# Small tables packed into one transfer, weights stored in the order they are read, early loads released one after another, and the weight scaling split over two engines

## The chip, the cores and the metric

The kernel runs on all 8 cores of one Trainium2 chip, each with its own prompt sequence and its own 16 of the 128 sample rows; the weights and constant tables are the same for all, and every core reads its own copy. A core has five engines with a queue each: PE (TensorE, matrix products into eight PSUM banks), DVE (VectorE), ACT (ScalarE), POOL (GpSimd) and SP (SyncE, which here only issues transfers). An engine runs its queue strictly in order, so an instruction that waits on a semaphore holds up all that stands behind it. Transfers are issued from SP's queue (no change of type) and from POOL's queue (those that turn f32 in HBM into bf16 on chip), and both share the core's 16 DMA engines. The metric is the device time in microseconds of the slowest core.

## The reference, cut to what matters

For 2048 prompt tokens (16 tiles of 128) after 16 learned meta tokens, and for 16 sample rows:

```python
hn   = rms_norm(h, norm_w)
proj = hn @ w_in                          # (1024) x (1024, 6144)
u, gp, q, k, v, gr = split(proj)          # six parts of 1024 columns
pool_o = group_linear(window_means(u) - u, w_pool) * pool_scale
ret_o  = retention(rotary(q), rotary(k), v)        # chunks of 128, state S
ret_y  = rms_norm_per_head(ret_o) * ret_norm_w * silu(gr)
pool_y = pool_o * silu(gp)
y = rms_norm(h + concat(pool_y, ret_y) @ w_out, final_norm_w)
```

## The kernel before

`build_program` records every piece of work with the buffers it reads and writes; `Prog.schedule` then lists the pieces per engine by a planner (ranks by remaining work, costs from small formulas, a DMA rate in `HBM`), and `Prog.place` inserts the waits. The order on each engine is therefore the planner's, and it changes when costs or dependencies change. A DMA that names a buffer among its *reads* is held until that buffer is written; this is used to hold a transfer back. `queue=` chains transfers in a fixed order.

`w_in` is read in 12 blocks of 512 columns (`load_w`, POOL's queue, 2 MB of f32 each, 1 MB on chip), in the order of `WORD`: blocks 10, 11, 6, 7, then 8, 9, 4, 5, then 2, 3, 0, 1. Blocks 0 and 1 make u, 2 and 3 gp, 4 and 5 q, 6 and 7 k, 8 and 9 v, 10 and 11 gr. Tile 0 is the sample rows and meta tokens together (48 rows); tiles 1 to 16 are the prompt.

The program has two phases. While the weights arrive, tiles 1, 0, 2, 3 and 4 (`order0`) are projected block by block (`pj_mm`, `gp_mm`), and retention (`att`) and pooling (`pool`) of tiles 1 to 3 are done in between. In this phase `norm_w` is applied to the transposed activations (`A2`, a DVE evacuation with `normw` as the scale). From tile 5 on the activations are transposed by DMA and not scaled; instead every block of `w_in_bf` is multiplied in place by `norm_w` (`fold_w`, eight DVE instructions for a block) once tiles 0 to 4 have used it, and the lower half of `w_out_bf` by `ret_norm_w` (`fold_w_out`). A projection of tile 5 has to wait for the folded block.

`w_out_bf` is used as scratch in the first phase (tiles x 1 to 3, gates, k, v), so its four blocks (`load_w_out`) are loaded when that scratch has been read, between two phases. `w_pool` and `pool_scale` are loaded to scratch (`scr`, `yT`), and one DVE multiply makes `w_pool_bf`, which `pool` needs. `outp(t)` is the output projection of a tile. After tile 5's start, each tile runs `head`, `att`, `pool`, `proj` and `outp` with PE nearly always busy.

Of the kernel before, what the change touches and what calls it, by code (L numbers as in the profile page):

```python
# [312 lines left out]
def build_program():  # L313
# [177 lines left out]
    w_in_v = w_in.rearrange("(kc p) n -> p kc n", p=128)  # L491
    w_out_v = w_out.rearrange("(kc p) n -> p kc n", p=128)

    def load_w(blk):
        dma("pool", w_in_bf[:, :, blk * 512:(blk + 1) * 512], w_in_v[:, :, blk * 512:(blk + 1) * 512],
            [], ["win%d" % blk], 1 << 21, queue="w")

    def load_w_out(b):
        dma("pool", w_out_bf[:, b * 4:(b + 1) * 4, :], w_out_v[:, b * 4:(b + 1) * 4, :],
            [], ["wo%d%s" % (i, z) for i in range(4 * b, 4 * b + 4) for z in ("", "b")], 1 << 21, queue="w")  # L500
# [715 lines left out]
```

How the kernel before makes its waits and increments, by code:

```python
        def run(e, name):  # L261
            for item in self.streams[name]:
                if item[0] == "wait":
                    e.wait_ge(self.sems[item[1]], item[2])
                else:
                    _, fn, semkey, inc = item
                    fn(e).then_inc(self.sems[semkey], inc)
```

## Time and profile before

| | us |
|---|---|
| median of 3 runs (lowest, highest) | 618.67 (618.12, 619.84) |
| the profiled execution, its time | 618.45 |
| its span (slowest core, core 5) | 616.9 |
| spans of all cores | 605.4 to 616.9 |
| PE busy, core 5 | 570.6 (93%) |
| DVE busy | 414.6 (67%) |
| ACT busy | 266.0 (43%) |
| POOL busy | 112.5 (18%) |

All times below are of core 5, in us from the start of its span. "Idle before" an instruction is what its engine waited just ahead of it, with the work that ended the wait. A landing time counts from the issue of a transfer to its completion.

### The profile page before, as it was taken

What the parts mean: (1) busy time and instruction counts of PE and PEld (TensorE: products, weight loads), DVE (VectorE), ACT (ScalarE), POOL (GpSimd) and SP (SyncE); (2) the same over time, 40 slices, a digit from 0 to 9 for tenths busy, and PEclk for the clock granted to TensorE, in tenths of its full rate; (3) what the DMA queues carried; (4) which work ended last, traced back from release to release, by engine and by line L of the source; (5) the groups of instructions that cost most, each with busy time, mean ns of one, the idle gap of its engine ahead of it and who ended that gap; (6) DMA issues with size and microseconds to landing.
All of it is one profiled execution on the core that took longest, in us unless ns stands there. A gap on an engine that the chain in (4) does not pass through costs nothing.

```text
span 616.9 us, 13819 instructions; the slowest of 8 cores (605.4 to 616.9 us)
## 1 busy us (share of the span) xinstructions
PE 570.6 (93%) x4360; PEld 313.9 (51%) x4360; DVE 414.6 (67%) x1114; ACT 266.0 (43%) x831; POOL 112.5 (18%) x131
## 2 busy tenths in 40 slices
PE   0699995999699999999999999999999999899994
PEld 0244452588354646555565646464454655455651
DVE  3349997477888755856676785867767673866463
ACT  2345463553333443343345344353644534355331
POOL 6300001121010111110011122322413310330010
PEclk9999997999899999999999999999999999999998
DMA  8999999486723542544263355575775635454621
GB/s 139 212 168 181 168 172 165 83 112 113 129 73 108 133 126 60 117 103 108 72 114 120 49 171 131 182 159 118 209 137 177 166 102 142 101 152 88 123 69 38
DMA packets 90034, 78.52 MB, mean 127 GB/s; under 512 B 56254, under 2 KB 72814, under 8 KB 89948
## 3 DMA queue, kind: packets, MB, share of 16 engines
q1 hardware_dynamic: 74524, 60.09, 39.5%
q0 software_dynamic: 15440, 17.55, 20.3%
q8 instruction: 37, 0.61, 0.4%
q14 instruction: 33, 0.27, 0.1%
HBM read 64.57 MB, written 18.41 MB: 135 GB/s over the span
## 4 chain that ended last, share of the span: by engine, by line
PE 82%; DMA 9%; DVE 3%; POOL 2%; issue 1%; another core or an unknown queue 1%; SPq 0%; DVEq 0%; POOLq 0%; ACT 0%; ACTq 0%
PE pp L588 42%; PE pp L863 20%; PE pp L603 8%; DMA w_in_bf<-w_in 6%; PE pp L837 2%; DMA w_out_bf<-w_out 2%; PE pp L929 2%; PE pp L916 1%; PE pp L818 1%; PE pp L748 1%; PE pp L707 1%; PE pp L724 1%; PE pp L750 1%; DVE w_in_bf L507 1%
## 5 line engine op out<-in xcount | busy, mean ns | idle before, releaser
L588 PE MATMUL pp<-w_in_bf,hnTs 128*128 128x512 bf16 x1120 | 260.9, 384 | 19.7 <-DMA w_in_bf<-w_in 18.2
L588 PEld LDWEIGHTS pp<-w_in_bf,hnTs 128*128 128x128 bf16 x1120 | 105.4, 99 | 144.3 <-issue 32.5
L863 PE MATMUL pp<-w_out_bf,yT 128*128 128x512 bf16 x448 | 102.2, 383 | 0.3
L623 ACT ACTIVATE F<-pp,dec 128x128 f32<-128x128 f32 (+1 forms) x216 | 61.7, 369 | 59.2 <-PE pp L588 54.1
L863 PEld LDWEIGHTS pp<-w_out_bf,yT 128*128 128x128 bf16 x448 | 43.1, 99 | 53.2 <-issue 4.0
L526 POOL TENSOR_TENSOR rs_r<-rs_r,nh 128x4 f32<-128x4 f32 x32 | 35.5, 1111 | 169.9 <-DVE rs_r L523 169.6
L603 PE MATMUL pp<-hnTs,w_in_bf 128*128 128x128 bf16 x896 | 53.5, 219 | 0.0
L603 PEld LDWEIGHTS pp<-hnTs,w_in_bf 128*128 128x128 bf16 x896 | 51.0, 98 | 3.4 <-issue 0.9
L872 ACT ACTIVATE pp<-xr 128x512 f32<-128x512 f32 x30 | 18.0, 601 | 74.5 <-DVE xr L870 64.5
L910 POOL TENSOR_TENSOR scr<-vM,ident 16x512 bf16<-16x512 bf16 x32 | 35.3, 1102 | 79.4 <-PE pp L916 76.0
L786 DVE SCALAR_TENSOR_TENSOR ry<-pp,rs_r,G 128x128 bf16<-128x128 f32 x104 | 29.2, 343 | 19.6 <-POOL rs_r L526 19.3
L870 DVE TENSOR_TENSOR xr<-xr,pp 128x512 f32<-128x512 f32 x30 | 20.6, 687 | 29.6 <-PE pp L863 29.4
L640 DVE TENSOR_TENSOR F<-F,cs 128x512 f32<-128x512 f32 x53 | 36.6, 691 | 4.7
L588 PE MATMUL pp<-w_in_bf,xr 128*128 128x512 bf16 (+1 forms) x160 | 37.7, 380 | 1.0 <-DVE xr L575 1.0
L776 ACT ACTIVATE ry<-pp 128x128 bf16<-128x128 f32 x128 | 33.4, 291 | 8.7 <-PE pp L750 8.1
L610 ACT ACTIVATE us<-pp 128x512 bf16<-128x512 f32 x32 | 19.1, 596 | 37.2 <-PE pp L588 37.2
L918 DVE SCALAR_TENSOR_TENSOR scr<-scr,pp 128x512 f32<-128x512 f32 x32 | 21.9, 683 | 15.6 <-PE pp L916 15.2
L636 DVE SCALAR_TENSOR_TENSOR F<-F,cs 128x256 f32<-128x256 f32 x53 | 22.7, 427 | 14.0 <-ACT F L623 11.7
L733 DVE SCALAR_TENSOR_TENSOR W<-pp,mask 128x128 bf16<-128x128 f32 x128 | 27.2, 282 | 5.8 <-PE pp L724 5.7
L526 POOL TENSOR_TENSOR rs_x<-rs_x,nh 128x1 f32<-128x1 f32 (+1 forms) x17 | 9.9, 581 | 115.2 <-DVE rs_x L523 108.7
L776 ACT ACTIVATION_READ_ACCUMULATOR ry<-pp 128x1 f32 x128 | 28.4, 222 | 0.0
L610 ACT ACTIVATE scr<-scr 128x512 bf16<-128x512 f32 x32 | 20.2, 633 | 16.6 <-PE pp L929 14.3
(167 smaller groups left out, 767.0 us busy)
## 6 DMA issues: line engine op xcount, KB each, us to landing
w_in_bf<-w_in POOLq DMA_DIRECT2D x12, 1024.0 KB, 54.8
scr<-S_in SPq DMA_DIRECT2D x32, 256.0 KB, 3.5
...
xr<-x SPq DMA_DIRECT2D x15, 512.0 KB, 3.8
y<-xr SPq DMA_DIRECT2D x15, 512.0 KB, 2.8
xA<-x SPq DMA_DIRECT2D x14, 512.0 KB, 4.4
w_out_bf<-w_out POOLq DMA_DIRECT2D x4, 1024.0 KB, 15.2
w_out_bf<-x SPq DMA_DIRECT2D x3, 512.0 KB, 7.4
```

The costliest lines, as they stand in the source:

```text
L526: P.op("pool", lambda e: e.tensor_tensor(out=rs[r0:r1, c0:c0 + n], in0=rs[r0:r1, c0:c0 + n], in1=nh[r0:r1, 0:n], op=ALU.pow), reads=[rsk, ...
L588: r = e.matmul(bk(b)[:T, :], lhsT=h.ap[:, kc * T:(kc + 1) * T], rhs=w_in_bf[:, kc, c0:c0 + 512], start=(kc == 0), stop=(kc == 7))
L603: r = e.matmul(bk(b)[:, i * T:(i + 1) * T], lhsT=w_in_bf[:, kc, D + fc * 128:D + (fc + 1) * 128], rhs=h.ap[:, kc * T:(kc + 1) * T], start= ...
L610: P.op("act", lambda e: e.activation(out=dst() if callable(dst) else dst, in_=src(), func=func), reads=sk, writes=dk, cost=c_act(1, n))
L623: r = e.activation(out=Fa.ap[:T, i * 128:(i + 1) * 128], in_=bk(b)[:T, i * 128:(i + 1) * 128], func=AF.Copy, scale=dec[:T, dslot * 8 + h:d ...
L636: e.scalar_tensor_tensor(out=f1[:, :, 0, :], in0=f0[:, :, 1, :], scalar=-1.0, in1=sinb, op0=ALU.mult, op1=ALU.mult)
L640: P.op("dve", lambda e: e.tensor_tensor(out=f0, in0=f0, in1=cosb, op=ALU.mult), reads=Fa.k + Fb.k + cs.k, writes=Fa.k, cost=c_dve(1, 512))
L733: r = e.scalar_tensor_tensor(out=W0[:, h * 128:(h + 1) * 128], in0=bk(b)[:, i * 128:(i + 1) * 128], scalar=float(GAM[h] ** -128.0), in1=ma ...
L776: r = e.activation(out=ry_t[:, h * 128:(h + 1) * 128], in_=bk(b)[:, i * 128:(i + 1) * 128], func=AF.Square, accum_out=ss_r[:, h:h + 1])
L786: r = e.scalar_tensor_tensor(out=ry_t[:, h * 128:(h + 1) * 128], in0=bk(b)[:, i * 128:(i + 1) * 128], scalar=rs_r[:, h:h + 1], in1=gb.ap[: ...
L863: r = e.matmul(bk(b)[:T, :], lhsT=yap[:, kc * st:kc * st + T], rhs=w_out_bf[:, kc, nt * 512:(nt + 1) * 512], start=(kc == 0), stop=(kc == 15))
L910: P.op("pool", lambda e, qd=qd: e.tensor_tensor(out=Rh.ap[0:NS, :].rearrange("p (s v) -> p s v", s=4), in0=vM_t[0:NS, h * 128:(h + 1) * 12 ...
```

## The change

Seven small tables become one f32 tensor of 128 x 496 (`c_pack`: the two norm weights, the decay factors, and identity, mask and band as bf16 pairs seen as f32), loaded by SP as its second transfer; the views of it are bitcast back. `w_in` and `w_out` are rearranged on the host so that each block holds, for each partition, 4096 consecutive f32 (16 KB) where it was eight pieces of 2 KB (`w_in`) or four of 4 KB (`w_out`). The rotary tables of the first five tiles are held until block 10 has landed, `w_pool` and `pool_scale` until block 0 (they waited for block 4), x of tile 5 until block 2. `fold_w` becomes two pieces, four chunks on DVE and four on ACT, each with its own key.

```diff
-    w_in_bf = P.sb("w_in_bf", [128, 8, 6 * D], BF16)
+    w_in_bf = P.sb("w_in_bf", [128, 12, 8, 512], BF16)
...
+    pack = P.sb("pack", [128, 496], F32)
+    normw = pack[:, 0:8]
+    retwc = pack[:, 8:16]
+    dec = pack[:, 16:48]
+    ident = pack[:, 48:112].bitcast(BF16)
+    mask = pack[:, 112:176].bitcast(BF16)
+    band = pack[:, 176:496].bitcast(BF16)
...
+    def wk(blk):
+        return ["win%d" % blk, "win%dd" % blk, "win%da" % blk]
     def load_w(blk):
-        dma("pool", w_in_bf[:, :, blk * 512:(blk + 1) * 512], w_in_v[:, :, blk * 512:(blk + 1) * 512],
-            [], ["win%d" % blk], 1 << 21, queue="w")
+        dma("pool", w_in_bf[:, blk, :, :].rearrange("p a b -> p (a b)"), w_in[blk], [], wk(blk), 1 << 21, queue="w")
...
     def fold_w(blk):
-        def f(e):
-            r = None
-            for kc in range(8):
-                w = w_in_bf[:, kc, blk * 512:(blk + 1) * 512]
-                r = e.tensor_scalar(out=w, in0=w, scalar1=normw[:, kc:kc + 1], scalar2=None, op0=ALU.mult)
-            return r
-        P.op("dve", f, reads=["normw", "win%d" % blk], writes=["win%d" % blk], cost=c_dve(8, 512, 4))
+        for eng, k0 in (("dve", 0), ("act", 4)):
+            def f(e, eng=eng, k0=k0):
+                r = None
+                for kc in range(k0, k0 + 4):
+                    w = w_in_bf[:, blk, kc, :]
+                    s = normw[:, kc:kc + 1]
+                    if eng == "act":
+                        r = e.activation(out=w, in_=w, func=AF.Copy, scale=s)
+                    else:
+                        r = e.tensor_scalar(out=w, in0=w, scalar1=s, scalar2=None, op0=ALU.mult)
+                return r
+            P.op(eng, f, reads=["normw", "win%d" % blk], writes=["win%d%s" % (blk, eng[0])],
+                 cost=1.1 if eng == "dve" else c_act(4, 512, ptr=1))
...
-    dma("pool", ident[:], c_ident[:, :], [], ["ident"], 1 << 16, queue="w")
     load_x(1, stage[1])
+    dma("sp", pack[:], c_pack[:, :], [], ["ident", "mask", "band", "dec", "normw", "retwc"], 1 << 18, queue="i")
...
-    for t in range(5):
-        load_cs(t)
...
     for b in WORD[0]:
         load_w(b)
-    dma("pool", mask[:], c_mask[:, :], [], ["mask"], 1 << 16, queue="w")
+    for t in (1, 0, 2, 3, 4):
+        load_cs(t, ["win%d" % WORD[0][0]])
...
-        w_pool.rearrange("g (cc p) d -> p g cc d", p=128), ["win4"], sc(0, 8).k, 1 << 20, queue="late")
-    dma("sp", yT_t[:].bitcast(F32), pool_scale[0:1, :].broadcast_to([128, D]), ["win4"], yTk, 1 << 19, queue="late")
+        w_pool.rearrange("g (cc p) d -> p g cc d", p=128), ["win0"], sc(0, 8).k, 1 << 20, queue="late")
+    dma("sp", yT_t[:].bitcast(F32), pool_scale[0:1, :].broadcast_to([128, D]), ["win0"], yTk, 1 << 19, queue="late")
...
-    load_x(5, xA)
+    load_x(5, xA, ["win2"])
```

The planner puts the instructions in a new order. On SP's queue the first rows before were these (`w_out_bf<-x` are x of tiles 1, 2 and 3 in scratch, `cs` and `xr<-c_cs` the rotary tables, `xA<-x` x of later tiles):

```order
L485 DMA w_out_bf<-x 128x1024
L485 DMA normw<-normw_col 128x8
L485 DMA dec<-c_dec 128x32
L485 DMA xA<-xs 16x1024
L485 DMA xA<-meta 16x1024
L485 DMA cs<-c_cs 128x128
L485 DMA xr<-c_cs 48x128
L485 DMA cs<-c_cs 128x128 x2
L485 DMA w_out_bf<-x 128x1024
L485 DMA cs<-c_cs 128x128
```

Now x of tile 2 comes fifth, and the five rotary tables, held for block 10, stand ahead of x of tile 3:

```order
L481 DMA w_out_bf<-x 128x1024
L481 DMA pack<-c_pack 128x496
L481 DMA xA<-xs 16x1024
L481 DMA xA<-meta 16x1024
L481 DMA w_out_bf<-x 128x1024
L481 DMA cs<-c_cs 128x128
L481 DMA xr<-c_cs 48x128
L481 DMA cs<-c_cs 128x128 x3
L481 DMA w_out_bf<-x 128x1024
L481 DMA xA<-x 128x1024 x2
L481 DMA cs<-c_cs 128x128 x2
L481 DMA scr<-w_pool 128x8x256
```

On DVE, the making of `w_pool_bf` stood here before, late in the first phase (`S_f` and `S_bf` are the retention state, the L636 to L642 rows rotary):

```order
L642 TENSOR_TENSOR qd<-w_out_bf 128x512
L642 TENSOR_TENSOR qd<-F 128x512
L762 SCALAR_TENSOR_TENSOR S_f<-S_f,pp 128x128 x8
L1032 TENSOR_TENSOR w_pool_bf<-scr,yT 128x2048
L636 SCALAR_TENSOR_TENSOR w_out_bf<-w_out_bf,cs 128x4x64
L638 TENSOR_TENSOR w_out_bf<-w_out_bf,cs 128x4x64
```

Now it stands behind the last rotary of tile 4, ahead of half a fold of block 4, the copies of the state and the last rotary sums:

```order
L636 SCALAR_TENSOR_TENSOR w_out_bf<-w_out_bf,cs 128x4x64
L638 TENSOR_TENSOR w_out_bf<-w_out_bf,cs 128x4x64
L640 TENSOR_TENSOR w_out_bf<-w_out_bf,cs 128x512
L1028 TENSOR_TENSOR w_pool_bf<-scr,yT 128x2048
L523 TENSOR_SCALAR rs_x<-ss_x 128x1
L506 TENSOR_SCALAR w_in_bf<-w_in_bf,pack 128x512 x4
L803 CAST S_bf<-S_f 128x512 x2
L642 TENSOR_TENSOR qd<-w_out_bf 128x512 x2
```

On PE, between the phases, tile 4's attention (L724 scores, L748 and L750 its output from the masked scores `W`) stood ahead of the first output projection (L863, tile 1) before:

```order
L603 MATMUL pp<-F,w_in_bf 128x128 x64
L588 MATMUL pp<-w_in_bf,F 128x512 x16
L588 MATMUL pp<-w_in_bf,hnTs 128x512 x8
L724 MATMUL pp<-qT,kT 128x128 x8
L588 MATMUL pp<-w_in_bf,hnTs 128x512 x8
L707 MATMUL pp<-v,kd 128x128 x8
L748 MATMUL pp<-v,W 128x128
L750 MATMUL pp<-S_bf,qT 128x128
...
L863 MATMUL pp<-w_out_bf,yT 128x512 x32
```

Now the output projection of tile 1 comes first, and two more groups of tile 4 (its gr, blocks 10 and 11) stand ahead of it:

```order
L603 MATMUL pp<-F,w_in_bf 128x128 x64
L588 MATMUL pp<-w_in_bf,F 128x512 x32
L588 MATMUL pp<-w_in_bf,hnTs 128x512 x8
L863 MATMUL pp<-w_out_bf,yT 128x512 x32
L724 MATMUL pp<-qT,kT 128x128 x8
L588 MATMUL pp<-w_in_bf,hnTs 128x512 x8
L748 MATMUL pp<-v,W 128x128
L750 MATMUL pp<-S_bf,qT 128x128
```

## Rows read from the trace of the kernel before

**Rows 1.** Stretches: length, busy time (count) of each engine, clock, DMA share

```profile
24.60:97.50 72.90, 71.26 (x408) 33.51 (x408) 57.19 (x162) 39.80 (x118) 4.27 (x5) 1.00 1.10 174
...
108.00:113.00 5.00, 5.00 (x18) 1.94 (x16) 0.00 (x0) 1.19 (x2) 0.00 (x0) 0.70 0.86 135
...
170.00:300.00 130.00, 130.00 (x923) 71.29 (x921) 90.71 (x233) 53.33 (x177) 14.58 (x19) 1.00 0.39 100
```

**Rows 2.** Timeline of PE at five places: start, length, work, idle before

```profile
19.59 3.19 PE L588 MATMUL pp<-w_in_bf,hnTs 128*128 128x512 bf16 x8 [9.09 <-DMA w_in_bf<-w_in]
...
24.63 1.89 PE L588 MATMUL pp<-w_in_bf,xr 128*48 128x512 bf16 x8 [1.00 <-DVE xr L575]
...
105.10 6.52 PE L588 MATMUL pp<-w_in_bf,hnTs 128*128 128x512 bf16 x16 [7.57 <-DMA w_in_bf<-w_in]
...
165.38 0.22 PE L748 MATMUL pp<-v,W 128*128 128x128 bf16 x1 [4.98 <-DVE W L733]
...
166.01 8.55 PE L863 MATMUL pp<-w_out_bf,yT 128*128 128x512 bf16 x32
```

**Rows 3.** Issues at 2.3, 6.3, 22, 67 and 146 us: size, landing

```profile
w_in_bf<-w_in POOLq DMA_DIRECT2D x1, 1024.0 KB, 17.2
...
w_out_bf<-x SPq DMA_DIRECT2D x1, 512.0 KB, 12.0
...
w_in_bf<-w_in POOLq DMA_DIRECT2D x1, 1024.0 KB, 83.0
...
scr<-w_pool SPq DMA_DIRECT2D x1, 1024.0 KB, 17.9
...
yT<-pool_scale SPq DMA_DIRECT2D x1, 512.0 KB, 21.4
...
w_out_bf<-w_out POOLq DMA_DIRECT2D x1, 1024.0 KB, 17.4
```

**Rows 4.** Timeline of DVE: `w_pool_bf`, folds of `w_in_bf` and `w_out_bf`

```profile
48.37 2.18 DVE L507 TENSOR_SCALAR w_in_bf<-w_in_bf,normw 128x512 bf16<-128x512 bf16 x8
...
103.14 2.29 DVE L1032 TENSOR_TENSOR w_pool_bf<-scr,yT 128x2048 bf16<-128x2048 f32 x1
...
156.25 1.67 DVE L517 TENSOR_SCALAR w_out_bf<-w_out_bf,retwc 128x1024 bf16<-128x1024 bf16 x4 [3.60 <-DMA w_out_bf<-w_out]
157.84 6.38 DVE L507 TENSOR_SCALAR w_in_bf<-w_in_bf,normw 128x512 bf16<-128x512 bf16 x24
```

**Rows 5.** DMA queues, 52:66 (two rows), 124:135, 143:156: packets, MB, share

```profile
q0 software_dynamic: 1872, 1.89, 99.5%
q1 hardware_dynamic: 144, 0.52, 12.5%
...
q0 software_dynamic: 528, 1.05, 51.6%
...
q0 software_dynamic: 607, 1.21, 65.6%
```

**Rows 6.** Timeline of the first 25 us, POOL, SP and DVE

```profile
1.58 0.73 POOL L485 DMA_DIRECT2D ident<-c_ident  x1 [0.88 <-POOLq L314]
...
2.31 3.54 POOL L485 DMA_DIRECT2D w_in_bf<-w_in  x4
...
6.31 0.86 SPq L485 DMA_DIRECT2D w_out_bf<-x  x1
...
7.23 0.65 POOL L526 TENSOR_TENSOR rs_x<-rs_x,nh 128x1 f32<-128x1 f32 x1
...
13.18 1.62 DVE L575 TENSOR_SCALAR hnTs<-pp,normw 128x128 bf16<-128x128 bf16 x8
...
20.70 0.75 DVE L544 TENSOR_SCALAR qd<-w_out_bf,rs_x 128x1024 bf16<-128x1024 f32 x1 [0.88 <-POOL rs_x L526]
...
23.19 1.29 DVE L575 TENSOR_SCALAR xr<-pp,normw 128x48 bf16<-128x48 bf16 x8 [1.74 <-PE pp L554]
```

**Rows 7.** Costliest groups of the page: busy, mean ns

```profile
L610 ACT ACTIVATE scr<-scr 128x512 bf16<-128x512 f32 x32 | 20.2, 633 | 16.6 <-PE pp L929 14.3
```

More of the change, by code:

```diff
@@ L326, in build_program @@
     pool_in = din("pool_in", [NS * 15, D])
-    normw_col = din("normw_col", [128, 8])
-    w_in = din("w_in", [D, 6 * D])
+    w_in = din("w_in", [12, 128, 8 * 512])
     w_pool = din("w_pool", [4, 256, 256])
     pool_scale = din("pool_scale", [1, D])
-    retw_col = din("retw_col", [128, 8])
-    w_out = din("w_out", [2 * D, D])
+    w_out = din("w_out", [4, 128, 4 * D])
     finw = din("finw", [1, D])
-    c_ident = din("c_ident", [128, 128])
+    c_pack = din("c_pack", [128, 496])
     c_cs = din("c_cs", [NT + 1, 128, 128])
-    c_dec = din("c_dec", [128, 32])
-    c_mask = din("c_mask", [128, 128])
-    c_band = din("c_band", [128, 640])
     c_csel = din("c_csel", [128, 192])
@@ L489, in tT @@
         return 128 if t else TM
[L491 to L492 removed]
+    def wk(blk):
+        return ["win%d" % blk, "win%dd" % blk, "win%da" % blk]
     def load_w(blk):
[L495 to L496 removed]
+        dma("pool", w_in_bf[:, blk, :, :].rearrange("p a b -> p (a b)"), w_in[blk], [], wk(blk), 1 << 21, queue="w")
     def load_w_out(b):
[L499 to L500 removed]
+        dma("pool", w_out_bf[:, b * 4:(b + 1) * 4, :].rearrange("p a b -> p (a b)"), w_out[b], [], ["wo%d%s" % (i, z) for i in range(4 * b, 4 * b + 4) for z in ("", "b")], 1 << 21, queue="w")
     def fold_w(blk):
[L503 to L509 removed]
+        for eng, k0 in (("dve", 0), ("act", 4)):
[11 more added lines that the diff above has]
+                 cost=1.1 if eng == "dve" else c_act(4, 512, ptr=1))
     def fold_w_out():
@@ L588, in mm @@
                 r = e.matmul(bk(b)[:T, :], lhsT=h.ap[:, kc * T:(kc + 1) * T],
-                             rhs=w_in_bf[:, kc, c0:c0 + 512], start=(kc == 0), stop=(kc == 7))
+                             rhs=w_in_bf[:, c0 // 512, kc, :], start=(kc == 0), stop=(kc == 7))
             return r
-        P.op("pe", mm, reads=h.k + ["win%d" % (c0 // 512)], writes=[b], cost=c_pe(8, 512))
+        P.op("pe", mm, reads=h.k + wk(c0 // 512), writes=[b], cost=c_pe(8, 512))
         return b
@@ L1162, in _constants @@
         band[32:32 + NMETA, 576 + gi * 16:576 + (gi + 1) * 16] = ((d3 <= w - 1) / w)[:, 0:16]
-    c["c_band"] = band
     csel = np.zeros((128, 2, 4, 16), np.float32)
@@ L1173, in _constants, with bits @@
             cu[s, gi, s] = 1.0 / w - 1.0
+    def bits(a):
+        u = np.ascontiguousarray(a).view(np.uint32) >> 16
+        return (u[:, 0::2] | (u[:, 1::2] << 16)).astype(np.uint32).view(np.float32)
+    c["c_pack"] = np.concatenate([c.pop("c_dec"), bits(c.pop("c_ident")), bits(c.pop("c_mask")), bits(band)], 1)
     c["c_csel"] = np.concatenate([csel.reshape(128, -1), cu.reshape(128, -1)], 1)
@@ L1189 @@
         "meta": f(meta_tokens),
-        "normw_col": f(np.asarray(norm_w, np.float32).reshape(8, 128).T),
-        "w_in": f(np.asarray(w_in)[0]),
+        "w_in": f(np.asarray(w_in)[0].reshape(8, 128, 12, 512).transpose(2, 1, 0, 3).reshape(12, 128, 4096)),
         "w_pool": f(np.asarray(w_pool)[0]),
         "pool_scale": f(np.asarray(pool_scale).reshape(1, D)),
-        "retw_col": f(np.asarray(ret_norm_w, np.float32).reshape(8, 128).T),
-        "w_out": f(np.asarray(w_out)[0]),
+        "w_out": f(np.asarray(w_out)[0].reshape(4, 4, 128, D).transpose(0, 2, 1, 3).reshape(4, 128, 4 * D)),
         "finw": f(np.asarray(final_norm_w).reshape(1, D)),
```

21 lines of the change are left out of this document (7 added, 14 removed).

## The prediction

> **What bounds the kernel now.** I read the page first, for the shares, then the stretches, then PE's timeline where it had waited, and then what it had waited for. PE is the bound: from 170 us on it is busy without a gap (130.00 of 130 us, [rows 1]), and both orders of work are nearly the same there, so whatever the change does it does in the first 170 us. There the reader is to see four losses on PE's own timeline.
> (1) The first weight group starts at 19.59, after 9.09 us of waiting for block 10, the first to land [rows 2].
> (2) The second group, tile 0's, starts only at 24.63, because tile 0's transposed activations come late [rows 2]. From there PE runs well: 71.26 us busy of 72.9 to 97.5 [rows 1], so 1.55 us of idle time.
> (3) At 97.53 it stands still for 7.57 us, for block 0, which lands 83.0 us after its issue at 22 [rows 2, 3]. Then the clock is low: granted 0.70 on average from 108 to 113 [rows 1], between its levels of 1.2 and 2.4 GHz, and 16 matmuls take 6.52 us where two groups of eight take 2 x 1.89 [rows 2], so 2.7 us go too. Together 10.3.
> (4) At 160.4 it waits 4.98 us for `W`, tile 4's masked scores [rows 2]. DVE is late with them: it waited 3.60 us for a block of `w_out` and then folded three blocks for 6.38 us [rows 4]. Afterwards 32 matmuls take 8.55 us, against 4 x 1.89 [rows 2]: 1.0 lost. Together 6.0.
>
> The sum is made against the profiled execution, 618.45 us (span 616.9, and 1.55 around it), 0.2 below the median of the runs.
>
> **The price of a weight block.** Of the layout no row shows the 16 KB pieces, so I price packets. A row's share times 16 engines times its stretch, over its packets, is the time of one. `w_in` now moves 2 KB of f32 per packet: 0.995 x 16 x 14 us / 1872 = 119 ns, and a block is 64 packets on each engine, 7.6 us. Pieces of 4 KB: x takes 0.125 x 16 x 14 / 144 = 194 ns, `w_out` 172 and 225 ns in two stretches, some 200 on average [rows 5]. At that price a block is 32 x 200 = 6.4 us. The bounds are no gain at all (7.6) and the line through both sizes carried on (81 ns for each further 2 KB, so 686 ns for 16 KB, eight of them 5.5 us). I take 6.4, the largest piece that a row shows, since `w_out` and x agree on it. The Trainium skill, "HBM Reference", section "Specifications (TRN2)", gives some 358 GB/s to each core when both cores of a pair read. No run here shows that limit by itself; as an estimate from it a block of 2.1 MB takes 5.9 us, and the sum below would come out at 600.
>
> **The start.** POOL no longer issues `ident` first (0.73 us, [rows 6]), so block 10 is issued at 1.58. It landed 17.2 us after its issue, with x of tiles 1 and 2, the sample rows and rotary tables beside it [rows 3]; the rotary tables (0.33 MB) are now held back and the pack (0.25 MB) has come in. Scaled with the block's price (6.4/7.6) the 17.2 become 14.5: it lands at 16. The price unchanged would make it 18.8. Tile 1 must be ready too: before, at 13.18 + 1.62 = 14.8 [rows 6]. POOL now issues nine blocks (0.89 us each, as four took 3.54, so until 9.6) ahead of tile 1's power, which stood at 7.23 [rows 6]; what followed it took 5.95 us to the evacuation, so tile 1 is ready between 14.8 and 17.2. Most of those 5.95 were a wait for tile 0's rows, so this stays hidden behind block 10, and would cost 1.2 if not.
> Tile 0's group needs its transposes, which stand behind the first group on PE (3.19 us, [rows 2]), and its evacuation, which stands behind tile 2's scaling on DVE. By the first path 16 + 3.2 + 0.5 + 1.3 = 21. By the second, x of tile 2 was issued at 6.31, landed 12.0 later and was scaled by 21.45 [rows 3, 6]; it now stands fifth on SP and not tenth, so some 1.3 us earlier, and the path ends at 21.6 or sooner. I take 21 for 24.63: **3.6 gained** (1.6 to 4.6). Then tiles 3 and 4 come no earlier than their x, and x of tile 3 now stands behind tables held for block 10: I add **1.0** of idle time, 2.5 in all in this stretch.
>
> **Block 0.** From 16 it takes ten blocks at 6.4, x of tiles 3 to 5 (8 packets per engine each at 194 ns, 4.7 in all) and the tables (1.0, an estimate): 85.7. Gone from this stretch are `w_pool`, `pool_scale` and the band table. PE asks for it after 34 groups and one small gate group, where before 37 were done at 97.53; that is 5.3 us of work less. So PE is there at 21 + 71.35 + 2.5 - 5.3 = 89.5, and block 0 has landed: **10.3 gained**, cover 3.8 us.
>
> **What is late next.** `w_pool` and `pool_scale` are issued when block 0 lands. Before they took 17.9 and 21.4 us [rows 3] beside `w_in`. Now block 1 (6.4) shares the engines, `w_pool` is 64 packets of 1 KB on each engine, at most 7.6 at 119 ns, and `pool_scale` 1.6: 15.6 in all, or 22 with the first `w_out` block as well. I take 17, near the lower end, as that block is issued only when tile 1's gate is read. So both are there at 102.7. The multiply that makes `w_pool_bf` (2.29 us, [rows 4]) waits for them on DVE, and behind it in the queue stand half a fold (1.09) and the copies of the state that PE's L748 of tile 2 needs: about 4 us. PE gets there after 41 groups, 8.2 us of work more than at the old 97.53: 21 + 71.35 + 2.5 + 8.2 = 103. It waits until 106.7: **3.7 lost**, and 1.0 for the clock as after the gap at 160.4. With both tables there by 99 nothing is lost.
>
> **Folds and the second gap.** DVE gives up half of 12 x 2.18 us [rows 4], 13.1. ACT takes 48 instructions; its nearest row is 633 ns [rows 7], so 30 us over a stretch in which it was busy about half the time (39.80 of 72.9, [rows 1]); I cost that at nothing, since its evacuations have several groups of slack in PSUM banks. PE now runs tile 1's output projection before tile 4's scores are used, so `W` is no longer late. The projection's second half needs the last `w_out` block instead: 17.4 us from issue to landing [rows 3] plus a fold of 1.67, against some 19 us of PE work between (eight groups, one of tile 5, half the projection): 0.5 waited. So 6.0 - 0.5 = **5.5 gained**. On ScalarE the Trainium skill, "ScalarE: Activation LUTs", section "Rules for kernel authors", says to leave multiplies to VectorE, which in bf16 is up to about three times as fast. The rows agree (633 ns against 2.18/8 = 273).
>
> **Sum**: -3.6 + 1.0 - 10.3 + 4.7 - 5.5 = -13.7, so 604.7 us.
>
> **The rivals.**
> *The new wait does not come (22 in 100).* At 5.5 us a block, block 0 lands at 76 to 77, the tables by 94, before PE wants them. Then the 4.7 go and the start gives 1.0 more: 599. For it: nothing in the rows shows a floor at 6.4. Against: one `w_out` stretch shows 225 ns.
> *The layout gives nothing, and the change ends slower (17 in 100).* At 7.6 a block 10 lands at 18.8, tile 0's group starts at 23.9, block 0 lands at 100.5 and PE wants it at 92.5: 8.0 and 2.7 lost, then the tables come 17 later, 4.8 and 1.0 more. The sum is -0.7 + 1.0 - 10.3 + 16.5 - 5.5 = +1.0, 619.5, and 624 if the tables take 22. It decides from a price of about 7.5 us on. For it: the DMA share is over 1 throughout [rows 1], with eight cores reading at once, and the 225 ns are nearly twice 119.
> *Long packets hold back SP's loads (10 in 100).* If x of tiles 2 to 4 waits behind 16 KB pieces, tile 0's and 2's groups come some 5 us later: 610. For it: x of tile 2 took 12.0 us beside `w_in` [rows 3]. Against: a block has an eighth of the pieces.
> *ACT's folds delay evacuations (6 in 100).* Eight folds of four instructions, 2.5 us each, stand among the evacuations between the phases; half a microsecond of each reaching PE gives 609.
>
> **How the numbers follow.** The case of the sum holds 45 in 100, between 599 and 611. The range 596 to 617 leaves out the lowest part of the first rival and most of the second, about 17 in 100. A measurement of this kernel can tell about 0.3%, 1.9 us. All cases but the second rival are faster; of that one about a third each is faster, the same or slower: 0.88, 0.06, 0.06.
>
> **What would show it.** The first weight group near 16 and tile 0's near 21; one packet row of `w_in` with an eighth of the packets; no PE wait on `w_in` near 100, but one of 2 to 6 us at L748 released by DVE, just after L1028, whose own wait is for the tables; no wait of 5 us at tile 4's L748; ACT some 30 us busier, DVE 13 less; the same PE time after 170. I am wrong if blocks still land 7.5 us apart, if PE waits for transposes of tiles 2 to 4 early on, or if the time comes from after the first 170 us.

## The result: 3.5% slower, and the profile after

The changed kernel takes 639.75 us (median of 4 runs, 638.20 to 641.03) and the kernel before 618.39 on the same chip: ratio 1.035, 95% interval 1.031 to 1.039. The forecast was 604.7. Some executions were disturbed on one die; all ratios leave them out, and where a median below would hold them I give the ratio times the median of before.

Core 3 is the slowest, with a span of 638.3 us. PE's own timeline in the first 70 us, the same view as [rows 2]:

```profile
16.32 3.57 PE L588 MATMUL pp<-w_in_bf,hnTs 128*128 128x512 bf16 x8 [6.11 <-DVE hnTs L575]
...
24.39 1.01 PE L554 MATMUL pp<-pack,qd 128*128 128x128 bf16 x8 [4.07 <-DVE qd L544]
25.59 2.85 PE L588 MATMUL pp<-w_in_bf,xr 128*48 128x512 bf16 x8 [0.19 <-DVE xr L575]
28.37 3.63 PE L588 MATMUL pp<-w_in_bf,hnTs 128*128 128x512 bf16 x16
61.10 1.01 PE L554 MATMUL pp<-pack,W 128*128 128x128 bf16 x8 [29.11 <-DVE W L544]
61.91 3.47 PE L588 MATMUL pp<-w_in_bf,hnTs 128*128 128x512 bf16 x8
```

The first group starts at 16.32, near the forecast of 16. Then PE stands still for 29.11 us in front of the transposes of tile 3 (`W` holds its normalized rows here). The release by DVE is only the last link. ACT's timeline gives the one before it, and the issues from 7.1 to 60 us (size, median us to landing) the first:

```profile
57.93 1.06 ACT L540 ACTIVATE W<-w_out_bf 128x1024 bf16<-128x1024 f32 x1 [35.10 <-DMA w_out_bf<-x]
```

```profile
w_out_bf<-x SPq DMA_DIRECT2D x1, 512.0 KB, 36.7
xA<-x SPq DMA_DIRECT2D x1, 512.0 KB, 43.5
cs<-c_cs SPq DMA_DIRECT2D x4, 64.0 KB, 23.2
xr<-c_cs SPq DMA_DIRECT2D x1, 24.0 KB, 14.7
```

So half a megabyte of x takes 36.7 us. Before, x of tile 3 was issued at 18.39, PE did not wait for it, and it took a fifth of that:

```profile
w_out_bf<-x SPq DMA_DIRECT2D x1, 512.0 KB, 7.4
```

Its place on SP now, from SP's timeline:

```profile
15.45 0.35 SPq L481 DMA_DIRECT2D cs<-c_cs  x1
15.85 0.84 SPq L481 DMA_DIRECT2D xr<-c_cs  x1
16.73 1.79 SPq L481 DMA_DIRECT2D cs<-c_cs  x3
21.18 0.33 SPq L481 DMA_DIRECT2D w_out_bf<-x  x1
21.78 0.44 SPq L481 DMA_DIRECT2D xA<-x  x1
```

It stands behind the five rotary tables, which the change holds until block 10 has landed. And what the two queues moved meanwhile (from 22 to 32, then from 32 to 45: packets, MB, share of 16 engines, as in [rows 5]):

```profile
q0 software_dynamic: 224, 1.65, 96.6%
q1 hardware_dynamic: 224, 0.10, 5.5%
...
q0 software_dynamic: 292, 2.13, 96.7%
q1 hardware_dynamic: 292, 0.13, 5.3%
```

This is the row to learn from: **224 packets against 224, 292 against 292.** q0 is the queue of `w_in`, q1 that of SP. They take turns, one packet each, and a packet of `w_in` now lasts 0.966 x 16 x 10 / 224 = 0.69 us on average, where it lasted 0.119 before [rows 5]. The sizes of the same packets, both queues together, from 22 to 32:

```profile
DMA packets 448, 1.75 MB, mean 175 GB/s; under 512 B 54, under 2 KB 246, under 8 KB 246
```

So 202 packets are of 8 KB. They are `w_in`'s whole pieces (16 KB of f32, 8 KB as bf16; 1.65 MB / 202 = 8.2 KB), and one takes some 0.966 x 16 x 10 / 202 = 0.76 us; the other 22 of that queue are tiny and draw the mean down to 0.69. SP's packets are small: 246 - 54 = 192 rows of a rotary table (0.10 MB / 192, about 512 B) and 32 tiny ones. But each waits for one of the other queue.

The waits before, for block 0 and at tile 4's scores, are gone. The stretches of after show where the time goes now (length, busy time and count of PE, PEld, DVE, ACT and POOL, clock, DMA share, GB/s):

```profile
32.00:45.00 13.00, 0.00 (x0) 0.00 (x0) 0.00 (x0) 0.00 (x0) 0.00 (x0) 0.59 1.02 174
45.00:58.00 13.00, 0.00 (x0) 0.00 (x0) 0.00 (x0) 0.07 (x1) 0.00 (x0) 0.50 0.99 195
58.00:72.00 14.00, 10.90 (x52) 4.88 (x53) 4.67 (x15) 7.12 (x17) 1.10 (x2) 0.75 1.02 181
72.00:98.00 26.00, 26.00 (x125) 11.36 (x124) 22.59 (x54) 17.67 (x47) 0.00 (x0) 1.00 0.65 122
98.00:113.00 15.00, 15.00 (x87) 7.07 (x85) 10.41 (x24) 7.70 (x25) 0.00 (x0) 1.00 0.02 5
113.00:130.00 17.00, 16.13 (x158) 9.65 (x155) 15.52 (x50) 12.70 (x43) 3.55 (x3) 1.00 0.52 128
```

From 32 to 58 no compute engine does anything to speak of, and the DMA engines are full: the weights stream in, unused. After that PE runs without a gap until 113, there is no wait for block 0, and from 98 to 113 the DMA share is 0.02, since the last block of `w_in` landed 75.0 us after its issue at 15.15. Before, that stretch held most of the 7.57 us wait, at a share of 1.07:

```profile
98.00:113.00 15.00, 7.90 (x24) 2.98 (x24) 7.33 (x19) 2.31 (x4) 0.80 (x1) 0.66 1.07 158
```

The clock fell to its lower level of 1.2 GHz in the idle time (granted 0.50) and was 0.75 from 58 to 72.

### The profile page after: what moved, and what is told of

Its sections match the earlier page's. It is cut to its first block, busy times and chain, and to the rows that moved or that the text cites. A ratio compares the mean times of both kernels' runs of the same rounds, so it can differ in the third digit from the quotient of the medians.

```text
span 638.3 us, 13813 instructions; the slowest of 8 cores (632.1 to 638.3 us)
## 1 busy us (share of the span) xinstructions
PE 571.9 (90%) x4360; PEld 315.9 (49%) x4360; DVE 403.1 (63%) x1066; ACT 293.5 (46%) x879; POOL 104.7 (16%) x128
## 4 chain that ended last, share of the span: by engine, by line
PE 76%; DMA 16%; DVE 3%; issue 2%; POOL 1%; ACT 1%; SPq 1%; DVEq 0%; POOLq 0%; ACTq 0%
PE pp L588 39%; PE pp L863 18%; DMA w_out_bf<-x 9%; PE pp L603 8%; DMA w_out_bf<-w_out 3%; PE pp L837 2%; DMA scr<-S_in 2%; PE pp L916 1%; PE pp L929 1%; PE pp L818 1%; PE pp L748 1%; PE pp L724 1%; PE pp L707 1%; PE pp L750 1%; PE pp L554 1%
## 5 line engine op out<-in xcount | busy, mean ns | idle before, releaser
L863 PE MATMUL pp<-w_out_bf,yT 128*128 128x512 bf16 x448 | 100.8, 379 | 2.6 <-DVE w_out_bf L517 2.1
L623 ACT ACTIVATE F<-pp,pack 128x128 f32<-128x128 f32 (+1 forms) x216 | 61.5, 370 | 57.2 <-PE pp L588 52.6
L863 PEld LDWEIGHTS pp<-w_out_bf,yT 128*128 128x128 bf16 x448 | 42.7, 98 | 55.0 <-issue 5.0
L603 PE MATMUL pp<-hnTs,w_in_bf 128*128 128x128 bf16 x896 | 54.8, 222 | 0.0
L910 POOL TENSOR_TENSOR scr<-vM,pack 16x512 bf16<-16x512 bf16 x32 | 35.2, 1100 | 98.9 <-PE pp L916 79.9
L786 DVE SCALAR_TENSOR_TENSOR ry<-pp,rs_r,G 128x128 bf16<-128x128 f32 x104 | 29.2, 343 | 19.8 <-POOL rs_r L526 19.7
L870 DVE TENSOR_TENSOR xr<-xr,pp 128x512 f32<-128x512 f32 x30 | 20.6, 687 | 25.0 <-PE pp L863 24.8
L523 DVE TENSOR_SCALAR rs_x<-ss_x 128x1 f32<-128x1 f32 (+1 forms) x17 | 2.5, 147 | 52.5 <-ACT W L540 32.0
L733 DVE SCALAR_TENSOR_TENSOR W<-pp,pack 128x128 bf16<-128x128 f32 x128 | 27.1, 280 | 6.9 <-PE pp L724 6.7
L636 DVE SCALAR_TENSOR_TENSOR F<-F,cs 128x256 f32<-128x256 f32 x53 | 23.2, 437 | 12.3 <-ACT F L623 10.0
L504 ACT ACTIVATE w_in_bf<-w_in_bf,pack 128x512 bf16<-128x512 bf16 x48 | 30.5, 717 | 0.0
## 6 DMA issues: line engine op xcount, KB each, us to landing
w_out_bf<-x SPq DMA_DIRECT2D x3, 512.0 KB, 15.2
```

The costliest lines, as they stand in the source:

```text
L504: r = e.activation(out=w, in_=w, func=AF.Copy, scale=s)
L603: r = e.matmul(bk(b)[:, i * T:(i + 1) * T], lhsT=w_in_bf[:, 2 + fc // 4, kc, fc % 4 * 128:(fc % 4 + 1) * 128], rhs=h.ap[:, kc * T:(kc + 1) ...
L623: r = e.activation(out=Fa.ap[:T, i * 128:(i + 1) * 128], in_=bk(b)[:T, i * 128:(i + 1) * 128], func=AF.Copy, scale=dec[:T, dslot * 8 + h:d ...
L636: e.scalar_tensor_tensor(out=f1[:, :, 0, :], in0=f0[:, :, 1, :], scalar=-1.0, in1=sinb, op0=ALU.mult, op1=ALU.mult)
L733: r = e.scalar_tensor_tensor(out=W0[:, h * 128:(h + 1) * 128], in0=bk(b)[:, i * 128:(i + 1) * 128], scalar=float(GAM[h] ** -128.0), in1=ma ...
L786: r = e.scalar_tensor_tensor(out=ry_t[:, h * 128:(h + 1) * 128], in0=bk(b)[:, i * 128:(i + 1) * 128], scalar=rs_r[:, h:h + 1], in1=gb.ap[: ...
```

## The experiments

Theory A: the queues take turns by packet, so each row that SP loads costs one packet of `w_in`. Theory B: the holds, the new places or the folds on ACT are at fault, whatever the layout. Theory C: SP is starved by bytes, and its number of rows does not matter. In the numbers of rows below, a transfer of 128 rows is taken as 8 rows on each of 16 engines and the table of 48 as 3: x of tile 3 has 4 x 8 + 3 = 35 rows of tables ahead of it and 8 of its own. Each ratio is to the kernel before. The diffs are cut: declarations, the host's rearranging and uses that follow from the lines shown are left out.

### The layout undone

```diff
-    w_in = din("w_in", [12, 128, 8 * 512])
+    w_in = din("w_in", [D, 6 * D])
...
-        dma("pool", w_in_bf[:, blk, :, :].rearrange("p a b -> p (a b)"), w_in[blk], [], wk(blk), 1 << 21, queue="w")
+        dma("pool", w_in_bf[:, blk, :, :], w_in.rearrange("(kc p) n -> p kc n", p=128)[:, :, blk * 512:(blk + 1) * 512], [], wk(blk), 1 << 21, queue="w")
```

> The change with w_in left in its old layout in memory, so that its packets carry 2 KB of f32 each again; every engine's order is that of the changed kernel. Theory A (the two DMA queues take turns packet by packet, so each row that SP loads costs one packet of w_in: 0.69 us now, 0.119 us before): x of tile 3, which took 36.7 us behind the held rotary tables, lands within 14 us, the 29.1 us of PE at 61.1 are gone or under 5, and the time is 612 to 624, with a wait for block 0 or w_pool near 95 to 110 in its place. Theory B (the held tables, the new places on SP and POOL or the folds on ACT are the loss, whatever the layout): x of tile 3 still takes over 25 us and the time stays above 633.

Ratio 0.992 (0.989 to 0.995), 613.3 us. Everything but the long pieces of `w_in` is kept (those of `w_out` too), and the loss becomes a gain of 4.9 us. PE's longest wait after 20 us, the landing of x of tile 3, and the queues from 24 to 40:

```profile
34.37 1.01 PE L554 MATMUL pp<-pack,W 128*128 128x128 bf16 x8 [6.54 <-DVE W L544]
```

```profile
w_out_bf<-x SPq DMA_DIRECT2D x1, 512.0 KB, 11.4
```

```profile
q0 software_dynamic: 1867, 1.88, 85.9%
q1 hardware_dynamic: 566, 1.17, 24.3%
```

The counts differ now: with packets of 0.118 us (0.859 x 16 x 16 / 1867) SP empties its queue, and `w_in` takes the turns that are left over. The wait of 6.54 us is a little over the "under 5" that I expected of theory A, and the wait for block 0 or `w_pool` that I expected in its place did not come: PE waits no longer than 0.9 us at a time from 35 to 129. Theory B is out as the explanation of the loss. But 6.54 of the 29.11 us are there with short pieces too, and before there was no wait at this place; so about 6.5 us come with the other edits, probably with the held tables ahead of x, and the long pieces made 29.1 of them.

### The tables in longer rows, and in shorter ones

Both leave the bytes, the place on SP and the orders of the other engines as they are. First one transfer with rows of 2 KB for tiles 1 to 4 (11 rows on each engine ahead of x, not 35):

```diff
-    for t in (1, 0, 2, 3, 4):
-        load_cs(t, ["win%d" % WORD[0][0]])
+    dma("sp", cs4[:, :], c_cs4[:, :], ["win%d" % WORD[0][0]], ["cs0", "cs1", "cs2", "cs3"], 1 << 18)
+    load_cs(0, ["win%d" % WORD[0][0]])
```

> The changed kernel with the four rotary tables of tiles 1 to 4 in one transfer with rows of 2 KB (128 rows in place of 512; the bytes and the place on SP are the same); the other engines' orders are unchanged. Theory A (each row of SP costs one w_in packet of 0.69 us): the tables are 11 rows on each engine and not 35, so x of tile 3 lands some 16 us sooner, about 20 us after its issue, PE's wait of 29.1 us shrinks to 11 to 15, and the time is 620 to 628. Theory C (SP's queue is starved by bytes, its row count does not matter): x of tile 3 still takes 33 us or more and the time stays above 635.

Ratio 1.0065 (1.0042 to 1.0088), 621.6 us; x of tile 3 takes 17.6 us and PE waits 10.0, both a little less than the 20 and 11 to 15 given. Then rows of 256 B, 70 on each engine:

```diff
-        dma("sp", csB[t].ap[:T, :], c_cs[t, 0:T, :], after, csB[t].k, 1 << 16, "d_cs%d" % (t % 4 if t else 4))
+        dma("sp", *((csB[t].ap[:T, :].rearrange("p (q d) -> p q d", q=2), c_cs2[t, :, 0:T, :].rearrange("q p d -> p q d")) if t < 5 else (csB[t].ap[:T, :], c_cs[t, 0:T, :])), after, csB[t].k, 1 << 16, "d_cs%d" % (t % 4 if t else 4))
```

> The changed kernel with the first five rotary tables stored and loaded in rows of 256 B, two for each of 512 B: the same bytes, the same place on SP, the orders of all engines unchanged. Theory A (a row of SP costs a packet of w_in, whatever it holds): 35 rows more on each engine at 0.85 us are 30 us more, x of tile 3 lands 62 to 70 us after its issue, PE's wait of 29.1 us becomes 54 to 64, and the time is 660 to 675. Theory C (SP gets a small share of the bytes): the same bytes, so x of tile 3 takes 36 to 40 us as before and the time stays at 637 to 645.

Ratio 1.0735 (1.0674 to 1.0796), 664.5 us. PE's wait, the landing, and the queues from 24 to 40:

```profile
84.97 1.01 PE L554 MATMUL pp<-pack,W 128*128 128x128 bf16 x8 [52.75 <-DVE W L544]
```

```profile
w_out_bf<-x SPq DMA_DIRECT2D x1, 512.0 KB, 61.5
```

```profile
q0 software_dynamic: 360, 2.63, 98.2%
q1 hardware_dynamic: 360, 0.08, 4.0%
```

One for one again, at half the bytes for SP (0.08 MB / 360 = 222 B on average). The same table bytes cost 17.6, 36.7 and 61.5 us by their number of rows alone: theory C is out. The differences give the price: (61.5 - 36.7) / 35 = 0.71 us a row, and (36.7 - 17.6) / 24 = 0.80, beside the packet's 0.69 on average and 0.76 for a whole piece. My expectation had 0.85, because I divided the whole 36.7 by 43 rows; some 5 us of it do not depend on the rows (x of tile 1, with little beside it, took 4.8). That is why PE's wait came out at 52.7, just under the 54 to 64 given.

### Pieces of 8 and of 4 KB

```diff
-    w_in = din("w_in", [12, 128, 8 * 512])
+    w_in = din("w_in", [12, 4, 128, 1024])
...
-        dma("pool", w_in_bf[:, blk, :, :].rearrange("p a b -> p (a b)"), w_in[blk], [], wk(blk), 1 << 21, queue="w")
+        dma("pool", w_in_bf[:, blk, :, :].rearrange("p (q a) b -> p q (a b)", q=4), w_in[blk].rearrange("q p n -> p q n"), [], wk(blk), 1 << 21, queue="w")
```

(for 8 KB with 2 in place of 4 and 2048 in place of 1024)

> The changed kernel with w_in stored so that a partition's piece is 8 KB of f32 and not 16; all orders the same. Theory A, now with a price: behind 35 table rows and 8 of its own on each engine x of tile 3 took 36.7 us with 16 KB pieces (0.85 us a row) and 11.4 us with 2 KB pieces (0.27 us a row). In between in proportion, 8 KB is some 0.5 us a row: x of tile 3 lands 20 to 23 us after its issue, PE waits 12 to 17 us for tile 3's transposes, and the time is 620 to 628. If instead only pieces of 16 KB hurt (a limit and not a price), x of tile 3 lands within 14 us and the time is under 616.

Ratio 1.0126 (1.0075 to 1.0177), 626.5 us; x of tile 3 takes 24.3 us and PE waits 19.3, both a little over what I gave (20 to 23 and 12 to 17), with the time inside its range. The queues from 24 to 40 are:

```profile
q0 software_dynamic: 603, 2.34, 87.2%
q1 hardware_dynamic: 609, 0.66, 16.6%
```

> The changed kernel with pieces of 4 KB for w_in; all orders the same. Theory A: 0.3 to 0.35 us a row, x of tile 3 lands 13 to 16 us after its issue, PE waits 7 to 10 us there, a block costs some 6.4 us in place of 7.6, and the time is 611 to 617, near the 613.6 of 2 KB pieces: what the row price costs, the block's price gives back. A limit and not a price: under 12 us, under 610.

Ratio 1.0005 (0.996 to 1.0049), 619.0 us; x takes 15.7 us, PE waits 8.6. The time is above the range that I gave. Then 4 KB pieces with the tables in rows of 2 KB, the two edits together:

> Pieces of 4 KB for w_in and the four rotary tables in one transfer with rows of 2 KB; all engines' orders but SP's one transfer as in the change. Theory A: 19 rows at 0.3 to 0.35 us, x of tile 3 lands 6 to 8 us after its issue, PE waits under 3 us for tile 3's transposes, and the time is 604 to 611. If the tables' rows do not count once pieces are short, it is that of 4 KB alone, 611 to 617.

Ratio 0.990 (0.984 to 0.996), 612.2 us; x takes 11.1 us, longer than my 6 to 8, PE waits 4.4 (under 3 given), and the time is 1 us above the range. The difference to 4 KB alone is (15.7 - 11.1) / 24 = 0.19 us a row. The queues of the kernel with 4 KB alone, from 24 to 40, put its packet at 0.791 x 16 x 16 / 1014 = 0.20:

```profile
q0 software_dynamic: 1014, 2.01, 79.1%
q1 hardware_dynamic: 695, 1.23, 27.7%
```

All seven kernels together; the packet is the mean of all packets of `w_in`'s queue, worked out from the queue rows as above:

| piece of `w_in` | packet, us | rows ahead + own | x of tile 3, us | PE's wait for it | time, us |
|---|---|---|---|---|---|
| 16 KB (the change) | 0.69 | 35 + 8 | 36.7 | 29.1 | 639.8 |
| 16 KB, tables of 256 B | 0.70 | 70 + 8 | 61.5 | 52.7 | 664.5 |
| 16 KB, tables of 2 KB | 0.69 | 11 + 8 | 17.6 | 10.0 | 621.6 |
| 8 KB | 0.37 | 35 + 8 | 24.3 | 19.3 | 626.5 |
| 4 KB | 0.20 | 35 + 8 | 15.7 | 8.6 | 619.0 |
| 4 KB, tables of 2 KB | 0.21 | 11 + 8 | 11.1 | 4.4 | 612.2 |
| 2 KB | 0.12 | 35 + 8 | 11.4 | 6.5 | 613.3 |

It is a price and not a limit. Each landing time less rows times packet leaves between 4.5 us (tables of 2 KB) and 8.4 us (8 KB): a fixed part, and a packet of `w_in` for each row. What x gains in landing the end gains: from the second line to the first 24.8 and 24.7 us, from the first to the third 19.1 and 18.2.

### x of tile 3 ahead of the tables

```diff
-    load_x(3, stage[3], stage[2].k)
+    load_x(3, stage[3], stage[1].k)
```

> The changed kernel with x of tile 3 issued together with x of tile 2, ahead of the held rotary tables, not behind its landing; the planner swaps a few neighbours in the orders. Theory A (turns by packet, the tables' 35 rows on each engine are what x of tile 3 waits behind): x of tile 3 lands near 28, so the wait for tile 3's transposes falls from 29.1 us to under 3; x of tile 4 still stands behind the tables and lands at 47 to 58, where PE then waits 5 to 15 us; the time is 618 to 630. Theory C (SP starved by bytes while w_in loads): x of tile 3 lands after 45 and the time stays above 633.

Ratio 1.040 (1.038 to 1.043), 643.2 us: no gain at all, against the 618 to 630 that I gave theory A. PE and ACT:

```profile
69.50 1.01 PE L554 MATMUL pp<-pack,sgp 128*128 128x128 bf16 x8 [24.11 <-ACT w_out_bf L610]
```

```profile
ACT sgp L540 <- DMA xA<-x: 35.1, 1, 35.1
```

x of tile 3 landed at 28.7, as expected, and 2.6 us of its wait are left. But x of tile 4 took its place: issued at 18.55, it took 47.3 us and landed at 65.9, 37.2 after x of tile 3. Those are the same 43 rows as the change's 36.7 us, moved on by one tile. I had the tables begin at 15.4; in fact they stood behind 16 rows of x as well. The mechanism held, my count for this kernel did not.

### The layout alone, put into the kernel before

```diff
-    w_in = din("w_in", [D, 6 * D])
+    w_in = din("w_in", [12, 128, 8 * 512])
...
-        dma("pool", w_in_bf[:, :, blk * 512:(blk + 1) * 512], w_in_v[:, :, blk * 512:(blk + 1) * 512],
-            [], ["win%d" % blk], 1 << 21, queue="w")
+        dma("pool", w_in_bf[:, blk, :, :].rearrange("p a b -> p (a b)"), w_in[blk],
+            [], ["win%d" % blk], 1 << 21, queue="w")
```

> The kernel before with w_in alone laid out in blocks of 16 KB per partition; all orders and holds are those of before. Theory A: the rotary tables, issued early and ahead of x of tile 2, make x of tile 2 land near 30 (18 before) and x of tile 3 near 42, PE loses 12 to 20 us for transposes before 50, the wait of 7.57 us for block 0 is gone, and the time is 617 to 630. Theory B (the holds and places are the loss and the layout itself is a gain): x of tile 2 lands by 19, the wait for block 0 goes, and the time is 604 to 612.

Ratio 1.055 (1.053 to 1.058), 651.6 us, worse than the whole change and than theory A's own range. PE's largest waits:

```profile
41.61 1.01 PE L554 MATMUL pp<-ident,qd 128*128 128x128 bf16 x8 [22.12 <-DVE qd L544]
...
62.87 1.01 PE L554 MATMUL pp<-ident,W 128*128 128x128 bf16 x8 [12.92 <-DVE W L544]
```

x of tile 2 took 31.8 us in place of 12.0 [rows 3], and x of tile 3 could be issued only then and took 21.2. There is no wait on `w_in` any more. 22.1 + 12.9 lost less the 10.3 of the block-0 gap make 24.7 of the 33.3 us; further waits of 2.6 and 3.8 us and the low clock behind each gap belong to the rest, which I did not follow to its end. With the same pieces x of tile 2 took 15.2 us in the change, where the tables stand behind it: their later place moved the damage behind tile 2.

### SP's rows taken out of the way

x of tiles 2 and 3 go into the queue of `w_in`, where they take no turns with it; pieces stay at 16 KB and the tables are in rows of 2 KB.

```diff
-    load_x(2, stage[2], stage[1].k)
-    load_x(3, stage[3], stage[2].k)
...
-    for b in WORD[0]:
+    for i, b in enumerate(WORD[0]):
         load_w(b)
+        if i < 2:
+            dma("pool", stage[i + 2].ap, x[(i + 1) * 128:(i + 2) * 128, :], [], stage[i + 2].k, 1 << 19, queue="w")
```

> Pieces of 16 KB as in the change, but x of tiles 2 and 3 stand in the queue of w_in, behind its first and its second block, and the four tables are one transfer with rows of 2 KB; the planner orders some groups of the first phase anew. Theory A: x no longer pays a w_in packet for each row, so both land by 26; x of tile 4, still on SP behind 11 rows, lands by 38, before PE wants it near 42; no wait of PE over 3 us between 26 and 100, and the time is what was forecast for the change without this loss, 600 to 608. If something else of the change costs the time (folds on ACT, the order), it stays above 612.

Ratio 0.993 (0.990 to 0.996), 614.7 us, above the 600 to 608 given. Both land by 26 (14.0 and 22.6 us after issues at 2.29 and 3.33), but x of tile 4 took 17.2 us on SP and PE waited 9.1 us for it at 37. So the tables go there too, behind the third block:

```diff
+        elif i == 2:
+            dma("pool", cs4[:, :], c_cs4[:, :], [], ["cs0", "cs1", "cs2", "cs3"], 1 << 18, queue="w")
...
-    for t in (1, 0, 2, 3, 4):
-        load_cs(t, ["win%d" % WORD[0][0]])
+    load_cs(0, ["win%d" % WORD[0][3]])
```

> The changed layout of 16 KB pieces with x of tile 2, x of tile 3 and the four tables (rows of 2 KB) in the queue of w_in behind its first, second and third block; on SP stand only x of tile 4 and tile 0's small table. Theory A: x of tile 4 pays 8 rows, some 7 us, and lands by 26, x of tiles 2 and 3 land by 17 and 26 as in the run before this one, PE waits for no transposes of tiles 2 to 4 longer than 2 us, and the time is 602 to 608, what the prediction gave without this loss. If the layout, the folds on ACT or the later wait for w_pool cost more than the prediction said, the time is above 610 with these waits gone.

Ratio 0.986 (0.982 to 0.990), 610.0 us: the fastest kernel with an interval here, 30 us less than the change, and 2 us above the range. PE at tile 4's transposes, on the slowest core:

```profile
35.14 1.01 PE L554 MATMUL pp<-pack,sgp 128*128 128x128 bf16 x8 [6.50 <-DVE rs_x L523]
```

and on a core whose span is 600.7 (610.1 on the slowest):

```profile
31.00 0.61 PE L554 MATMUL pp<-pack,sgp 128*128 128x128 bf16 x8 [1.69 <-DVE rs_x L523]
```

x of tile 4 took 14.1 us on the one and 11.0 on the other, for 8 rows: 8 x 0.69 and 5.5 to 8.6 us besides. So the 2 us of waiting at most that I gave held on the one core and not on the other. With 4 KB pieces in the same kernel (the edit of above):

> The kernel with x of tiles 2 and 3 and the four tables in the queue of w_in, now with pieces of 4 KB in place of 16; all orders as there. What was left there was x of tile 4 on SP: 8 rows took 14.1 us and PE waited 6.5 us on the slowest core, 1.7 on another. Theory A: at some 0.3 us a row x of tile 4 takes 6 to 9 us, PE waits under 2 us for its transposes, and the time is 602 to 607, under the 610 there and near the forecast for the change. If the rest is not SP's rows (the layout's own loss, blocks that come later with 4 KB), the time stays at 609 or above with a wait for w_in in its place.

Two times can be compared, 608.4 and 609.9: above the 602 to 607 given and too few for an interval, so I can't say that it is faster than with 16 KB. x of tile 4 no longer holds PE: it took 8.6 us on core 3 (span 605.9) and PE did not wait for it. In its place the wait for `w_pool_bf` appears, which the prediction had. On core 3 `w_pool` and `pool_scale` took 17.4 and 18.1 us to land, and DVE and then PE wait:

```profile
105.74 2.29 DVE L1029 TENSOR_TENSOR w_pool_bf<-scr,yT 128x2048 bf16<-128x2048 f32 x1 [4.96 <-DMA yT<-pool_scale]
```

```profile
113.67 0.61 PE L724 MATMUL pp<-qT,kT 128*128 128x128 bf16 x8 [3.88 <-DVE ry L786]
```

Between the two DVE works without a pause down to the L786 that PE waits for.

### The folds

All folds back on DVE, in the kernel with the tables behind the third block:

```diff
-        for eng, k0 in (("dve", 0), ("act", 4)):
+        for eng, k0 in (("dve", 0), ("dve", 4)):
```

> The kernel just described with all folds of w_in on DVE, in two halves of four, none on ACT; the planner orders some work anew. The prediction's step on the folds (13.1 us taken from DVE hide in ACT's idle time and end the wait for tile 4's scores, 5.5 us): 3 to 8 us slower than with the split, with DVE releasing PE late between 100 and 175. If the split did nothing, within 2 us of it.

Ratio 0.994 (0.991 to 0.998) against 0.986 with the split: 5.3 us slower, the size expected. But the place is another one, in the main:

```profile
93.90 5.50 PE L588 MATMUL pp<-w_in_bf,xr 128*128 128x512 bf16 x15 [7.28 <-ACT w_out_bf L623]
...
158.19 0.22 PE L748 MATMUL pp<-v,W 128*128 128x128 bf16 x1 [1.32 <-DVE W L733]
```

ACT stood there for 9.98 us behind x of tile 5, issued at 77.66 in place of 71.75. And x of tile 4 took 8.8 us there and not 14.1, with 1.3 us of waiting in place of 6.5. So the 5.3 us are not shown to be DVE's folding; tile 4's scores cost 1.3 of it.

## Why the prediction was wrong

**The step that failed** is in the start: x of tile 2 "stands fifth on SP and not tenth, so some 1.3 us earlier", and for tile 3 "x of tile 3 now stands behind tables held for block 10: I add 1.0". I priced SP's loads by their order of issue. What sets their time is the number of rows ahead, times the packet that they alternate with, which the layout made 5.8 times as long on average. x of tile 2 took 15.2 us and not 12.0, and the 1.0 was 29.1. The prediction named the sign itself: it is wrong "if PE waits for transposes of tiles 2 to 4 early on".

**The rival had the mechanism and the wrong size.** "Long packets hold back SP's loads" gave 610 and 10 in 100; the time was 640. It had tile 0's group some 5 us late, which came (4.6), and not the 29.1 us at tile 3. Its argument against, "a block has an eighth of the pieces", is the wrong way round: a row of SP waits for one piece, so fewer and longer pieces make each row dearer. I had read the sharing from 52 to 66, when SP had little to send (144 packets against 1872, [rows 5]). From 12 to 18, while SP's first loads waited, the trace of before has nearly as many packets of the one queue as of the other, which could have hinted at the turns:

```profile
q0 software_dynamic: 573, 0.58, 68.3%
q1 hardware_dynamic: 504, 0.65, 43.4%
```

The Trainium skill, "DMA: Bandwidth & Descriptors", section "Queues, rings and completion order", says that each DMA engine goes round the queues that have work, a packet at a time. The rows of 224 against 224 packets agree. The same section of the Trainium skill gives a packet some 9 to 17 descriptors as typical. In these rows the turn passed after every packet of the profile, be it one row of SP or one whole piece of `w_in`.

**The start.** The first group came at 16.32 (forecast 16), which is in part luck: block 10 had landed at 15.4, and the last wait was for tile 1's evacuation (6.11 us, L575). With 2 KB pieces the group came at 16.95, released by block 10:

```profile
16.95 3.57 PE L588 MATMUL pp<-w_in_bf,hnTs 128*128 128x512 bf16 x8 [4.08 <-DMA w_in_bf<-w_in]
```

So of the 3.3 us gained here on the 19.59 of before the long pieces of `w_in` gave 0.6, where the prediction had put down 2.8 to them (16 against 18.8). Tile 0's came at 25.59 (forecast 21), since the transposes of tile 2 stand ahead of it on PE and x of tile 2 was late: 4.6 off. (The pack that is loaded beside them holds six tables, as the diff shows, not seven.)

**Block 0.** The wait is gone, here and in the kernels with SP's rows taken away. But it is gone with 2 KB pieces as well, where the second rival still had it: that rival gave 619.5 for a layout without effect, and the run took 613.3, although PE lost 6.54 us at tile 3. So the gain is not shown to be the layout's. Blocks land 6.8 us apart with 16 KB pieces (15.4 for the first to 90.1 for the last, forecast 6.4) and 7.4 with 2 KB (16.8 to 97.9). A whole piece takes 0.76 us, near the 0.8 that I took; that the mean of all packets, 0.69, meets the line through both sizes (0.686) is chance.

**The new wait for `w_pool`** (4.7 us) did not come in after, but not for the first rival's reason, which had the two tables there by 94. They were issued only at 119.83 and 120.27, behind the rotary tables of later tiles on SP (block 0 had landed at 84.9), landed by 130.4, and DVE came to its multiply only at 134.49, as everything was late by then. In the kernel with 16 KB pieces and the rotary tables behind the third block they were issued at 93.07 and 94.02, took 8.2 and 10.0 us, not 17, and DVE came at 109.06; PE waits no longer than 0.2 us at a time from 36 to 119. With 4 KB pieces there, where PE loses nothing to x of tile 4, the wait came much as forecast: 17.4 and 18.1 us to land, and 3.88 us of PE on core 3 (forecast 17, and 3.7 before the clock).

**Folds.** ACT's folds are 717 ns each, where the nearest row had 633 [rows 7]:

```profile
L504 ACT ACTIVATE w_in_bf<-w_in_bf,pack 128x512 bf16<-128x512 bf16 x48 | 30.5, 717 | 0.0
```

ACT is busy for 293.5 us (266.0 before) and DVE for 403.1 (414.6): the 30 more and 13 less of the prediction, nearly. PE's longest wait on one of ACT's evacuations after 20 us is 0.87 us in after.

**Second gap.** The 4.98 us at tile 4's L748 are gone in after; of the half microsecond forecast for the output projection, 2.1 were waited (`w_out_bf`, L517). That it was the folds that ended the gap is not shown: the one run on it, with all folds on DVE, has 1.32 us at this place and not 4.98, and it changed x of tile 5 as well.

**The sum by the runs.** 604.7 + 29.1 (tile 3) + 4.6 (tile 0's group) + 2.0 (eight transposes and eight matmuls after the gap: 1.01 + 3.47 against the 0.61 and 1.89 of the same at the higher clock) + 1.0 (25.59: 2.85 against 1.89) - 4.7 (`w_pool`) + 1.6 (`w_out`) - 1.0 (the idle time added) = 637.3, against 639.9 for the profiled execution.

Open: with the waits for x nearly gone, the kernels here end at 608 to 610 and not at 604.7. With 16 KB pieces the slowest core still loses 6.5 us to x of tile 4, with 4 KB pieces a core loses 3.9 to `w_pool_bf`; what is left beyond it was not followed. No run has 2 KB pieces with SP's rows out of the way, so what the long pieces are worth by themselves is not shown, nor what the packed tables or the longer pieces of `w_out` are.
